# Streaming-encoder trunk: 28 instead of 24 seven-product quads in the down projection, half of their weight sums on GpSimd, and row factors and forget biases taken off TensorE

## The reference, cut to what matters

```
x = x + rmsnorm(hybrid_mixer(rmsnorm(x, g0), ...), g1)      # 16 heads in groups A, B, C
x = x + rmsnorm(memory_xattn(rmsnorm(x, g2), rmsnorm(mem, gm)), g3)
x = x + rmsnorm(conv_ffn(rmsnorm(x, g4), ...), g5)

# group B of the mixer, 6 heads of 128, frame-causal
log_f = log_sigmoid(fb + b_forget);  cum_f = cumsum(log_f, axis=tokens)
s_b   = q_b @ k_b.T * 128**-0.5 + cum_f[q] - cum_f[k]
p_b   = softmax(where(k <= q, s_b, -1e30))

# conv_ffn: u = h @ w_up (2048 x 8192), causal depthwise convolution of width 3,
y = (gelu(gate) * val) @ w_down                              # 4096 x 2048
```

## Time and profile before

| | before |
|---|---|
| median of 3 runs | 1981.32 us (1980.58 to 1981.58) |
| the profiled execution's own time | 1979.98 us |
| its span in the trace | 1978.2 us |
| PE busy | 1960.5 us, 10679 matmuls |
| DVE busy | 1505.7 us |
| ACT busy | 1139.7 us |
| POOL busy | 173.3 us, 199 instructions |
| raw loads | 640 of 512 KB, 4.2 us from issue to landing |

### The profile page before, as it was taken

One profiled execution on the slowest core, in us unless ns is written; L12 is line 12 of the kernel. 1 busy time (PEld: TensorE's weight loads), 2 busy tenths in 40 slices (PEclk: granted clock), 3 DMA queues, 4 the chain that ended last, 5 costly groups with the idle time before them and its releaser, 6 DMA issues.

```text
span 1978.2 us, 30768 instructions
## 1 busy us (share of the span) xinstructions
PE 1960.5 (99%) x10679; PEld 1685.6 (85%) x10679; DVE 1505.7 (76%) x2324; ACT 1139.7 (58%) x1774; POOL 173.3 (9%) x199
## 2 busy tenths in 40 slices
PE   9999999999999999999999999999999999999998
PEld 8888888888888888788798888888888888887886
DVE  7957677857777777788876577768587777778888
ACT  7755466656555555465576655556565555555554
POOL 0000000001222222100000000000012222221000
PEclk9999999999999999999999999999999999999999
DMA  8564567545666666576646444665446666565773
GB/s 322 195 188 149 170 209 244 194 151 170 194 199 204 200 208 189 202 264 243 225 145 209 153 156 150 216 213 195 156 153 208 202 203 201 195 205 194 257 257 135
DMA packets 110754, 391.81 MB, mean 198 GB/s; under 512 B 12800, under 2 KB 14208, under 8 KB 109312
## 3 DMA queue, kind: packets, MB, share of 16 engines
q1 hardware_dynamic: 105632, 368.36, 57.1%
q10 hardware_dynamic: 4448, 20.58, 2.7%
q0 software_dynamic: 576, 1.57, 0.4%
HBM read 380.24 MB, written 10.22 MB: 197 GB/s over the span
## 4 chain that ended last, share of the span: by engine, by line
PE 96%; DVE 3%; issue 1%; ACT 1%; POOL 0%; POOLq 0%; DVEq 0%; ACTq 0%
PE ps L959 24%; PE ps L962 12%; PE ps L873 11%; PE ps L875 11%; PE ps L874 11%; PE ps L885 11%; PE ps L888 5%; PE ps L1274 2%; PE ps L1276 2%; PE ps L1275 2%; PE ps L837 1%; DVE w_lo L1752 1%; PE ps L1225 1%; PE ps L1210 0%; PE ps L1213 0%
## 5 line engine op out<-in xcount | busy, mean ns | idle before, releaser
L1752 DVE TENSOR_TENSOR w_lo<-raw,w_hi 128x1024 fp32r<-128x1024 f32 (+2 forms) x660 | 777.6, 1187 | 324.2 <-ACT w_hi L1331 317.8
L1331 ACT ACTIVATE w_hi<-raw 128x1024 fp32r<-128x1024 f32 (+2 forms) x660 | 672.0, 1028 | 339.5 <-PE ps L962 219.3
L959 PE MATMUL ps<-h_t,w_hi 128*128 128x512 f32 x2032 | 638.9, 396 | 0.0
L962 PEld LDWEIGHTS ps<-h_t,w_lo 128*128 128x128 f32 x2032 | 381.9, 188 | 89.9
L962 PE MATMUL ps<-h_t,w_lo 128*128 128x256 f32 x2032 | 399.1, 278 | 0.0
L959 PEld LDWEIGHTS ps<-h_t,w_hi 128*128 128x128 f32 x2032 | 309.3, 189 | 0.0
L885 PE MATMUL ps<-h_t,w_hi 128*128 128x512 f32 x768 | 245.0, 400 | 0.0
L888 PEld LDWEIGHTS ps<-h_t,w_lo 128*128 128x128 f32 x768 | 144.3, 188 | 33.9
L2471 POOL TENSOR_SCALAR up_c<-up_u,cw 128x256 f32<-128x256 f32 x128 | 125.0, 988 | 377.3 <-DVE up_u L2328 377.3
L888 PE MATMUL ps<-h_t,w_lo 128*128 128x256 f32 x768 | 151.3, 278 | 0.0
L873 PE MATMUL ps<-w_hi,act_t 128*128 128x512 f32 x320 | 124.9, 390 | 0.1
(11 more groups left out here) (366 smaller groups left out, 2873.3 us busy)
## 6 DMA issues: line engine op xcount, KB each, us to landing
raw<-stream SPq DMA_DIRECT2D x640, 512.0 KB, 4.2
comb<-comb_hbm SPq DMA_DIRECT2D x24, 512.0 KB, 4.9
comb_hbm<-comb_out ACTq DMA_DIRECT2D x14, 512.0 KB, 6.2
raw<-stream SPq DMA_DIRECT2D x24, 288.0 KB, 3.5
raw<-stream SPq DMA_DIRECT2D x16, 262.0 KB, 3.1
gain_a<-gains_in ACTq DMA_DIRECT2D x4, 1024.0 KB, 6.5
m_x<-mem_t_in ACTq DMA_DIRECT2D x2, 2048.0 KB, 9.7
x<-x_in SPq DMA_DIRECT2D x4, 512.0 KB, 12.9
```

The source lines that it names most:

```text
L959: pe.matmul(ps[:, 4 * half + nt, :], hi[:, cc, nt * P:(nt + 1) * P], h_t[:, c, :, :], start=(c == 0), stop=False, skip_group_check=True)
L962: mm = pe.matmul(ps[:, 4 * half + nt, SEQ:2 * SEQ], lo[:, cc, nt * P:(nt + 1) * P], h_t[:, c, 0, :], start=False, stop=(c == KC - 1), skip ...
L1331: act.activation(w_hi[:, slot, 0:width], raw[:, rslot, 0:width], ACT.Copy).then_inc(hi_ready, 1)
L1752: dve.tensor_tensor(w_lo[:, slot, 0:width], raw[:, rslot, 0:width], w_hi[:, slot, 0:width].bitcast(F32), ALU.subtract).then_inc(lo_ready, 1)
```

## The change

1. `SEVEN` has a seventh member (12), so 14 quads a layer instead of 12 take seven products. The order is new, with two such quads directly after each other at two places in each pass.
2. The sums have two buffers (`psum_b[0]` and `psum_b[1]`). `first_sums` stays on DVE, two splits ahead, or in the quad ahead where two stand together. The two halves of C are made by GpSimd. The `raw` slots of such a quad are released by C's low part.
3. The last up group's tail runs ahead of the splits at chosen places (`tail_at`).
4. The merges are cut differently: group 2q+1 of the first pass is merged at its end (`merge_odd`) and not ahead of its last pieces. Between the layers the squares and gains of group 2 come one split later.
5. The factors `h1` and `mem` go through HBM on GpSimd's DMA queue (`factor_row`); their matmuls and ACT copies are gone. `h2` and `h3` stay.
6. The forget bias: the cumulated row goes through HBM and comes back as `f_k` and `f_q`, and DVE adds `f_k - f_q + mask` in two operations a head, which replaces the extra matmuls and the making of `fa` and `fb`.

```diff
-SEVEN = [0, 2, 4, 6, 8, 10]
-PASS_HEAD, PASS_MID, PASS_TAIL = [1, 3], [0, 5, 2, 7, 4, 9, 6, 11, 8, 13, 10], [12, 14, 15]
+SEVEN = [0, 2, 4, 6, 8, 10, 12]
+PASS_HEAD, PASS_TAIL = [1, 3], [[14, 15], [13, 14, 15]]
+PASS_MID = [[5, 0, 7, 2, 4, 9, 6, 8, 11, 10, 13, 12], [0, 5, 2, 4, 7, 6, 8, 9, 10, 11, 12]]
...
-    at(11 if layer else 14, ("R", "h1"))
...
-    at(P_OUT + 22, ("R", "mem"))
...
-        psum_b = sb("psum_b", [P, 4, 512], 88 * K)
+        psum_b = [sb(f"psum_b{i}", [P, 4, 512], at) for i, at in enumerate((88 * K, 104 * K))]
...
+        def tail_at(s):
+            return {P_DOWN + 4: 0, P_DOWN + 6: 2, P_DOWN + 10: 3, P_DOWN + 11: 4, P_DOWN + 12: 5, P_DOWN + 16: 6}.get(s, 1)
...
-                                    pe.matmul(dst, qb_t[:, h, q], kb_t[:, h, 0:nk], start=True, stop=False)
-                                    mm = pe.matmul(dst, fa[:, q], fb[:, h, 0:nk], start=False, stop=True)
+                                    mm = pe.matmul(dst, qb_t[:, h, q], kb_t[:, h, 0:nk], start=True, stop=True)
...
+                            if hk == "B":
+                                dve.wait_ge(f_got, 32 * (l + 1))
+                                for tb, (o, nk) in enumerate(((0, P), (P, SEQ))):
+                                    ins = dve.scalar_tensor_tensor(s[:, o:o + nk], f_k[:, h, 0:nk], f_q[:, h, tb:tb + 1],
+                                                                   mask_b[:, o:o + nk], ALU.subtract, ALU.add)
...
                 for s in range(P_DOWN + SPL, NSPLITS + (2 if l < DEPTH - 1 else 0)):
-                    if s == P_DOWN + SPL:
-                        first_sums(SEVEN_AT[0])
-                        other_sums(SEVEN_AT[0])
+                    up_tail(UPG // 2 - 1, 1, tail_at(s))
                     split_down(s)
-                    if s < P_DOWN + SPL + 8:
-                        up_tail(UPG // 2 - 1, 1, s - P_DOWN - SPL)
...
-                    if s + 2 in SEVEN_AT:
+                    if s + 2 in SEVEN_AT and s - 2 not in SEVEN_AT:
                         first_sums(s + 2)
-                    if s + 1 in SEVEN_AT:
-                        other_sums(s + 1)
+                    if s in SEVEN_AT and s + 4 in SEVEN_AT:
+                        first_sums(s + 4)
...
+                def factor_row(n, src, dst, here):
+                    pool.dma_start(r_hbm[n].rearrange("(t p) -> p t", p=P), src[:], allow_slow_non_contiguous=True).then_inc(r_put, 16)
+                    pool.wait_ge(r_put, 16 * (n + 1))
+                    pool.dma_start(dst[:], r_hbm[n].partition_broadcast(P)).then_inc(here, 16)
...
+                for n, s in enumerate(SEVEN_AT):
+                    ra, rb = [(P_DOWN + DOWN_SPLITS[s - P_DOWN + d][4]) % RAW for d in range(2)]
+                    m = l * len(SEVEN_AT) + n
+                    pool.wait_ge(b_sums, m + 1)
+                    sums = psum_b[n % 2]
+                    pool.tensor_tensor(sums[:, 2, :], sums[:, 0, :], raw[:, rb, 512:1024], ALU.add).then_inc(b_more, 1)
+                    pool.wait_ge(b_more, 2 * m + 1)
+                    pool.tensor_tensor(sums[:, 3, :], sums[:, 2, :], raw[:, ra, 512:1024], ALU.add).then_inc(b_more, 1)
```

More of the change, by code:

```diff
@@ L92 @@
             DOWN_RAW.append((2 * _q + _g, _j))
-    for _j in PASS_MID:
+    for _j in PASS_MID[_q]:
         for _g in (0, 1):
@@ L98 @@
                 DOWN_SPLITS.append(("N", _q, _j, 2 * _q + _g, len(DOWN_RAW)))
-            DOWN_FREED.append(len(DOWN_SPLITS) - 1)
+            DOWN_FREED.append(len(DOWN_SPLITS) - 1 if _j not in SEVEN else len(DOWN_SPLITS) + 2 - _g)
             DOWN_RAW.append((2 * _q + _g, _j))
@@ L103 @@
     for _g in (0, 1):
-        for _j in PASS_TAIL:
+        for _j in PASS_TAIL[_q]:
             DOWN_SPLITS.append(("N", _q, _j, 2 * _q + _g, len(DOWN_RAW)))
@@ L628, in build @@
         lf_ready = sem("lf_ready")
-        fab_ready = sem("fab_ready")
+        f_summed = sem("f_summed")
+        f_put = sem("f_put")
+        f_got = sem("f_got")
+        r_put = sem("r_put")
+        r_got = sem("r_got")
+        rm_got = sem("rm_got")
         s_ready = sem("s_ready")
@@ L753, in build @@
         comb_hbm = nc.dram_tensor("comb_hbm", (DEPTH * COMBS, P, 4 * 2 * P), F32, kind="Internal").ap()
+        f_hbm = nc.dram_tensor("f_hbm", (DEPTH, H_B, SEQ), F32, kind="Internal").ap()
+        r_hbm = nc.dram_tensor("r_hbm", (DEPTH + 1, SEQ), F32, kind="Internal").ap()
         bias_hbm1 = nc.dram_tensor("bias_hbm1", (4 * H_A, 4, 8 * SEQ), F32, kind="Internal").ap()
@@ L1309, in _ @@
                         take_acc(G_DOWN + k)
[L1310 to L1312 removed]
+                    if q == 1 and j == PASS_TAIL[q][0] and k % 2 == 1:
+                        pe.wait_ge(odd_merged, 2 * l + q + 1)
+                    if s >= NSPLITS - (2 if l < DEPTH - 1 else len(PASS_TAIL[q])):
                         continue
@@ L1394, in split_down @@
                         n = l * len(SEVEN_AT) + seven(s - 2 if kind == "B" else s - 3)
-                        act.wait_ge(b_sums, 3 * n + (1 if kind == "B" else 3))
+                        if kind == "B":
+                            act.wait_ge(b_sums, n + 1)
+                        else:
+                            act.wait_ge(b_more, 2 * n + 2)
                         act.wait_ge(split_free, l * NSPLITS + s + 1)
                         c = 0 if kind == "B" else 2
-                        act.activation(w_hi[:, s % SPL, :], psum_b[:, c:c + 2, :].rearrange("p a n -> p (a n)"),
+                        act.activation(w_hi[:, s % SPL, :], psum_b[n % 2][:, c:c + 2, :].rearrange("p a n -> p (a n)"),
                                        ACT.Copy).then_inc(hi_ready, 1)
@@ L1450, in t_evac_lo, with y_squares @@
                     act.activation(t_lo[:], ps[:, 2 * acc_slot(l, g):2 * acc_slot(l, g) + 2, SEQ:2 * SEQ], ACT.Copy).then_inc(t_lo_ready, 1)
-                def y_squares(g, yk):
+                def y_squares(g, yk, tbs=range(TB)):
                     group_done(g)
                     if yk in (8, 10):
-                        act.wait_ge(end_merged, 2 * l + (yk - 8) // 2 + 1)
+                        act.wait_ge(even_merged, 2 * l + (yk - 8) // 2 + 1)
+                    if yk == 9:
+                        act.wait_ge(odd_merged, 2 * l + 1)
                     if yk > 0:
-                        act.wait_ge(y_sq, l * 24 + 2 * yk)
-                    for tb in range(TB):
+                        act.wait_ge(y_sq, l * 24 + 2 * yk + tbs[0])
+                    for tb in tbs:
                         if tb == 1:
@@ L1600, in _ @@
                         b = read_bank(step)
-                        free_bank(act.activation((rm_t if step[1] == "mem" else r_t)[:], b[:, 0:SEQ], ACT.Copy), step)
+                        free_bank(act.activation(r_t[:], b[:, 0:SEQ], ACT.Copy), step)
                     elif kind == "osq":
@@ L1896, in split_down @@
                         c = 0 if kind == "B" else 2
+                        n = seven(s - 2 if kind == "B" else s - 3)
                         dve.wait_ge(hi_ready, l * NSPLITS + s + 1)
-                        dve.tensor_tensor(w_lo[:, s % SPL, :], psum_b[:, c:c + 2, :].rearrange("p a n -> p (a n)"),
+                        dve.tensor_tensor(w_lo[:, s % SPL, :], psum_b[n % 2][:, c:c + 2, :].rearrange("p a n -> p (a n)"),
                                           w_hi[:, s % SPL, :].bitcast(F32), ALU.subtract).then_inc(lo_ready, 1)
```

124 lines of the change are left out of this document (63 added, 61 removed).

## The result

The changed kernel takes 1987.37 us (median of 8 runs, 1987.15 to 1987.58), the kernel before 1981.45 us on the same chip (8 runs, 1980.58 to 1981.87). The ratio is 1.003, 95% interval 1.002 to 1.0041: slower by 0.3%. The prediction had 1980.9 us, no change that can be told, and a range of 1965 to 1993.

The account below looks back on a forecast made before the run. PE, busy 99% of the span, was taken to bound the kernel. Span 1978.2 - 15.1 saved + 14.7 given back = 1977.8, plus 3.1 to the median: 1980.9 us, range 1965 to 1993.

Parts of the forecast that it names:

- forget bias and factors: Matmuls removed from PE for 12 group B heads' forget bias and four factors: 2.8 and 1.8 us saved.
- old waits and turn: PE's waits for C's low part, once a layer, gone (7.1 us); shorter chain between the layers (0.7 us).
- given back in the down pass: New PE waits at B and C of paired seven-product quads because GpSimd's sums hold DVE: 14.7 us.
- I take h = 0.94, near the doubled hold: DVE time one 512-column GpSimd sum costs, put at 0.94 us from rows of 256-column additions.
- 4h - 2.17: PE's wait at each pair of seven-product quads, h being DVE's cost per GpSimd sum: 1.6 us, eight pairs, 12.7 us.
- The tail's part: Up group's tail in the chain of each layer's first pair: 1.0 us more a layer, 2.0 in all.
- The bound of h = 1.20: Upper bound of DVE's cost per GpSimd sum, if POOL's whole 0.72 us doubles: 24 us given back.
- The case with h = 1.20: Rival: long hold at the pairs, 24 us, and falling clock; 1986 to 1995, middle 1990, chance 0.20.
- GpSimd does not hold DVE up: Rival: GpSimd's sums cost DVE nothing or little; 1966 us, half effect 1971 to 1976, chance 0.33 together.
- DVE keeps the port while its queue is full: Rival: POOL's sums wait for DVE's idle time, at C of 20 or more quads; 30 us, 1997, chance 0.10.
- The hand-over at the end of the first pass: Rival: group 1's merge, squares and gain must fit 5.44 us; failure costs 1 to 2 us twice, no chance given.
- busy sum of PE lower by 7 us: Sign expected in the profile after: PE's busy time falls by about 7 us.

Follow-up runs that it names:

- down12: Changed kernel with 12 alternating seven-product quads a layer, all sums on DVE, and the kernel before's factor rows and forget bias: 1971.96 us.
- dve14: Changed kernel with the third and fourth sums of each quad back on DVE, 14 quads and pairs kept: 1970.85 us.
- dve12: Changed kernel with 12 alternating seven-product quads a layer and all four sums on DVE: 1967.07 us, ratio 0.9932 to the kernel before.
- pool12: Changed kernel with 12 alternating seven-product quads a layer, sums still on GpSimd: 1969.87 us.
- adds2: dve12 plus two GpSimd 128x512 additions per quad (10 of 12 quads a layer) whose results nobody reads: 1984.54 us.
- mixer: Kernel before with only the change's factor rows and forget bias, down pass as before: 1974.73 us.

## Why the prediction was wrong

The mechanism was right in place and count (16 waits at B and C of eight quads); a size was off, and it decided the sign. Against the prediction's steps:

| step | forecast, us | runs |
|---|---|---|
| forget bias and factors | 2.8 + 1.8 = 4.6 | 4.9, from two pairs of kernels |
| old waits and turn | 7.1 + 0.7 = 7.8 | 8.9 (before - down12); 9.5 from 1981.45 |
| 12 matmuls | 2.7 | not measured by itself; 2.7 by rows of 0.227 each |
| given back in the down pass | 14.7 | 6.5 + 16.5 = 23.0 |
| change of the median | about 0 | +5.9 |

The last but one row: dve14 is 3.8 us above dve12 although it has 12 matmuls less, so the pairs cost 3.8 + 2.7 = 6.5 us even with all sums on DVE. GpSimd adds 1987.37 - 1970.85 = 16.5. By the trace of the changed kernel the sum is 2 x 11.0 = 22.0, so about 1 us between the two accounts is open. That the time came within 6.5 us of the forecast is partly luck: the cost was put 8.3 us too low and the gains about 2 too low.

**The step that failed** is "I take h = 0.94, near the doubled hold": it made the term "given back" 14.7 us where the runs show 22 to 23. The rows showed an addition of 256 columns: it ended 0.59 us behind DVE's end, and in another place DVE was let in 0.19 ahead of POOL's end. I doubled the difference, 0.40, which with the lost overlap makes 0.88; the 0.06 up to 0.94 had no row at all. But only the first is work and grows with the columns. At 857.64 POOL's addition of 512 columns ends at 859.79, 1.15 us behind the split's end at 856.29 + 2.35 = 858.64 (twice 0.59 is 1.18). The next split ends at 856.29 + 4.58 = 860.87 and needs 1.22, so it was let in at 859.65, 0.14 ahead of POOL's end. The head start does not grow. 1.15 - 0.14 + 0.08 = 1.09, measured 1.14 in distances. The rows at hand would have given 2 x 0.59 - 0.19 + 0.08 = 1.07. The prediction's own formula then holds: 4h - 2.17 is 2.39 instead of 1.6 us a pair, 2.2 to 2.5 measured; eight pairs give 18 to 19, not 12.7. The tail's part gave back 3.6 instead of 2.0, and mostly by another way: I had counted its product and its low half in the chain of C, while 1.3 of the 1.8 us a layer (those that pool12 has too) come ahead of that, at A and at a plain piece, from additions that stop the convolution and a split. The prediction did not have these.

**The bound of h = 1.20** was nearer. It came from doubling POOL's whole 0.72 to 1.44, and an addition of 512 columns takes 1.29 alone, so it lay a little high. The Trainium skill's GPSIMD Engine Reference (section 3.1) gives 2.2 ns a column; by it, as an estimate, 256 columns more make 0.56 us and 0.72 + 0.56 = 1.28, and the trace agrees. The case with h = 1.20 stood at 1990, from 1986 to 1995, with a chance of 0.20. The result lies in it, and its 24 us of cost fit the 23.0; its other half, waits that bring the clock down, did not come. The granted clock is 1.00 over the pairs, with waits of up to 1.3 us.

**The rivals.** "GpSimd does not hold DVE up" is refuted by the rows at 856.29 and by adds2. "DVE keeps the port while its queue is full" is refuted by the same rows: L2508 gets in between two splits that follow each other directly, the second with its high part ready 1.4 us before. The hand-over at the end of the first pass did not fail: PE shows no extra distance over 0.05 us between the pairs of the first pass and those of the second (868 to 927 us), nor does dve12. The late biases did not come: PE has no wait in the mixer for `s_sb`.

**A sign that misled.** The prediction asked for a busy sum of PE lower by 7 us; it is lower by 3.0 only, with all 52 matmuls gone. In dve12 it is lower by 7.1 with 40 gone. The reading that fits, not tested by itself: a matmul beside a wait is counted with 0.39 to 0.50 us where one in a stream adds 0.227, so that new waits put back part of the busy time. For a kernel bound by PE, distances between starts are the measure.

## What to carry to other kernels

In these runs, moving an addition from SBUF off VectorE and onto GpSimd did not relieve VectorE: beside its stream of operations with two SBUF inputs, 0.69 us of work became 1.14 us of standing still. It could pay only where GpSimd runs while VectorE is idle, which no run here tried. So before such a move, compare the hold with what the operation costs on VectorE, and look for the stretch with the least slack: 20 additions cost 1.5 us and the next 20 cost 16.0. When a hold is scaled up from a smaller shape, separate the part that grows with the columns from the fixed hand-over, and try the edits of a bundle one by one: here the good ones (13.5 us together, with 12 quads in alternation) were hidden under one bad pairing.

## What the runs showed of the hardware

- A waiting addition on GpSimd went in at the end of VectorE's operation even when VectorE's next one was ready, and VectorE's next one after it, one for one (2.15 us for 1.29 of work on GpSimd, 2.28 for 1.14 on VectorE).
- GpSimd fills of 128x512 (527 ns) did not lengthen VectorE's operations beside them (median 684 ns, and 1967.11 us with them against 1967.07); additions from SBUF did (1780 ns).
- The operation that stands still need not be one of the kind that the wait is blamed on: PE's waits in adds2 are charged to the splits, which kept 1.22 us, while two sums ahead of them stood.
- The kernels that keep the wait of 2.4 us at C spread over 2.4 us and more from run to run (before 1979.3 to 1982.0, mixer 1974.5 to 1976.8), the others over 0.3 to 0.8. The spread goes with the mean granted clock of the run. The 39 runs of the kernel before fall in three groups that do not overlap: 0.999 with 1979.33 to 1979.65 us (6 runs), 0.998 with 1980.08 to 1980.59 (9), 0.997 with 1980.83 to 1981.99 (24). Mixer's nine do the same: 0.999 up to 1974.73, 0.998 at 1975.71 and 1976.02, 0.997 at 1976.41 and 1976.84. In mixer's profile, a run at 0.998, the clock falls behind this wait in the second layer and not in the first, as in the profile of the kernel before (also 0.998):

```profile
832.00:836.00 4.00, 3.45 (x14) 2.54 (x15) 3.49 (x5) 3.06 (x4) 0.00 (x0) 1.00 0.21 59
...
1812.00:1816.00 4.00, 3.75 (x11) 2.76 (x12) 3.49 (x5) 3.06 (x5) 0.00 (x0) 0.71 0.23 76
1816.00:1820.00 4.00, 4.00 (x16) 3.22 (x16) 3.96 (x6) 1.65 (x3) 0.00 (x0) 0.86 0.87 317
```

  (1 - 0.57) x 4 us is 0.001 of the span, so falls in none, one or both layers would give just these three clocks. That fits all the runs, but there are profiles of the middle group alone, and why the fall comes in one run and not in the next stays open. It would also account for most of the difference between 8.9 us and the 7.8 forecast: the forecast took one fall from a profile at 0.998, while the medians of the kernel before lie at 0.998 to 0.997, and down12 has none (all four runs at 0.999).
